# Turning the samples' attention sums by four transposes a head, with their quarters added in pairs by VectorE

## The reference, cut to what matters

```
s = einsum('bhik,bhjk->bhij', qc, kc) * w_intra
num = w_inter[..., None] * einsum('bhik,bhkv->bhiv', qc, C) + einsum('bhij,bhjv->bhiv', s, vc)
den = w_inter * einsum('bhik,bhk->bhi', qc, n) + sum(s, axis=-1)
h = num / maximum(abs(den), exp(-m_row))[..., None]
...
out = (sigmoid(o) * h_normed_by_head) @ w_out
```

## Time and profile before

| | |
|---|---|
| median of 3 runs | 2425.05 us (2423.37 to 2425.56) |
| time of the profiled execution | 2424.56 us |
| its span in the trace | 2422.4 us |
| PE busy, share of the span | 99% |
| DVE busy | 48% |
| ACT busy | 36% |
| POOL busy | 21% |
| granted TensorE clock, mean | 1.00 |

### The profile page before, as it was taken

The page is one execution under the profiler, slowest core; times in us unless marked ns, Lnnn a source line. Parts: engine busy times, 40 slices in busy tenths (PEclk is TensorE's granted clock), DMA queues, the critical chain, the costliest instruction groups (busy, mean ns, idle before and its releaser), DMA issues. The chain is left out here.

```text
span 2422.4 us, 43057 instructions
## 1 busy us (share of the span) xinstructions
PE 2409.2 (99%) x16236; PEld 2364.8 (98%) x16236; DVE 1160.7 (48%) x1332; ACT 877.0 (36%) x1048; POOL 509.6 (21%) x624
## 2 busy tenths in 40 slices
PE   9999999999999999999999999999999999999998
PEld 9999999999999999999988899999999999999997
DVE  6644444444434455544467875443444344434354
ACT  6333233333323333322445553333233333323332
POOL 7520022012101333210322113320022012101331
PEclk9999999999999999999999999999999999999999
DMA  6644554455445444545588764554554455445443
GB/s 237 176 150 151 151 148 148 148 149 153 147 147 149 149 144 147 146 145 152 160 275 270 250 194 139 157 148 150 152 149 148 148 149 152 149 147 148 147 152 113
DMA packets 198694, 389.68 MB, mean 161 GB/s; under 512 B 12229, under 2 KB 12485, under 8 KB 198153
## 3 DMA queue, kind: packets, MB, share of 16 engines
q1 hardware_dynamic: 197664, 385.78, 51.7%
q0 software_dynamic: 960, 2.94, 0.4%
HBM read 366.47 MB, written 22.66 MB: 161 GB/s over the span
## 5 line engine op out<-in xcount | busy, mean ns | idle before, releaser
L1108 DVE TENSOR_TENSOR w_lo<-w_raw,w_hi 128x1024 fp32r<-128x1024 f32 x648 | 829.4, 1282 | 1174.8 <-ACT w_hi L791 1157.9
L791 ACT ACTIVATE w_hi<-w_raw 128x1024 fp32r<-128x1024 f32 x608 | 644.4, 1061 | 1301.5 <-PE G L1589 1274.2
L1587 PE MATMUL G<-op_hi,w_hi 128*128 128x320 f32 x2816 | 873.6, 310 | 0.4 <-DVE qkv L1495 0.4
L1588 PE MATMUL G<-op_lo,w_hi 128*128 128x320 f32 x2816 | 868.6, 308 | 0.0
L1589 PE MATMUL G<-op_hi,w_lo 128*128 128x320 f32 x2816 | 868.6, 308 | 0.0
L1587 PE MATMUL G<-a_hi,w_hi 128*128 128x320 f32 x2304 | 710.9, 309 | 1.4 <-DVE hT L1227 0.8
L1589 PE MATMUL G<-a_hi,w_lo 128*128 128x320 f32 x2304 | 710.1, 308 | 0.0
L1588 PE MATMUL G<-a_lo,w_hi 128*128 128x320 f32 x2304 | 710.1, 308 | 0.0
L1587 PEld LDWEIGHTS G<-op_hi,w_hi 128*128 128x128 f32 x2816 | 528.2, 188 | 4.2 <-issue 1.3
L1588 PEld LDWEIGHTS G<-op_lo,w_hi 128*128 128x128 f32 x2816 | 528.2, 188 | 2.5 <-issue 1.0
L1589 PEld LDWEIGHTS G<-op_hi,w_lo 128*128 128x128 f32 x2816 | 528.1, 188 | 0.0
(11 more groups left out here) (253 smaller groups left out, 889.1 us busy)
## 6 DMA issues: line engine op xcount, KB each, us to landing
w_raw<-in_ffn_w_up SPq DMA_DIRECT2D x256, 512.0 KB, 3.7
w_raw<-in_ffn_w_down SPq DMA_DIRECT2D x256, 512.0 KB, 3.8
w_raw<-in_mlstm_w_in SPq DMA_DIRECT2D x96, 512.0 KB, 3.9
w_raw<-in_mlstm_w_out SPq DMA_DIRECT2D x32, 512.0 KB, 3.9
cst<-in_state_mlstm_C SPq DMA_DIRECT2D x26, 512.0 KB, 4.7
out_C_sample<-cst SPq DMA_DIRECT2D x26, 512.0 KB, 3.4
w_raw<-in_pool_w SPq DMA_DIRECT2D x8, 512.0 KB, 11.2
w_raw<-in_state_mlstm_C SPq DMA_DIRECT2D x6, 512.0 KB, 4.3
```

The source lines that it names most:

```text
L791: act.activation(w_hi[:, c % RING], w_raw[:, c % RING], ACT.Copy).then_inc(w_hi_ok, 1)
L1108: v.tensor_tensor(w_lo[:, slot], w_raw[:, slot], w_hi[:, slot].bitcast(F32), ALU.subtract).then_inc(w_lo_ok, 1)
L1587: pe.matmul(G[:, m, 0:T], w_hi[:, slot, t, w], hi[:, k, :], start=first and t == 0, stop=False)
L1588: pe.matmul(G[:, m, 0:T], w_hi[:, slot, t, w], lo[:, k, :], start=False, stop=False)
```

## The change

`samples_turned` no longer multiplies with `fold`. It transposes each 128 columns of `hs` against the identity, so that `X[2]` gets 4 blocks of 128 features by 128 columns (four quarters of 32) in place of 4 blocks of 64. `samples_out` takes the quarters apart: for each of the two parities (n = 0, 1) it copies the first quarter to `qkv` and adds the second quarter to it, and then multiplies by `rds` in place. A new semaphore, `fold_ok`, orders these steps. `fold` and its drawing on POOL go.

```diff
-        fold = sb("fold", [P, NS])
...
+        fold_ok = sem("fold_ok")
...
-            link(pool.memset(fold[:, :], 0.0))
-            for quarter in range(4):
-                select(by_quarter(fold[:, :])[:, quarter // 2], [[-TS, NSEQ // 2], [-1, TS]], 1, base=-quarter * GP,
-                       op=ALU.not_equal, fill=1.0)
...
             def samples_out(h):
 
                 v.wait_ge(x2_turned, h + 1)
-                v.tensor_tensor(att(h)[:, :, TP:T], X[2][:, 0:4 * NS].rearrange("p (a t) -> p a t", t=NS),
-                                bc(rds[:, :], [P, 4, NS]), ALU.mult).then_inc(att_s, 1)
+                turned = X[2][:, :].rearrange("p (a v t w) -> p v t a w", v=2, t=2, w=GP)
+                to = att(h)[:, :, TP:T].rearrange("p a (u v i) -> p v a u i", v=2, i=TS)
+                for n in range(2):
+                    first, second = (turned[:, n, t].rearrange("p a (u i) -> p a u i", i=TS) for t in range(2))
+                    v.tensor_copy(to[:, n], first).then_inc(fold_ok, 1)
+                    v.wait_ge(fold_ok, 4 * h + 2 * n + 1)
+                    v.tensor_tensor(to[:, n], second, to[:, n], ALU.add).then_inc(fold_ok, 1)
+                v.wait_ge(fold_ok, 4 * h + 4)
+                v.tensor_tensor(att(h)[:, :, TP:T], att(h)[:, :, TP:T], bc(rds[:, :], [P, 4, NS]), ALU.mult).then_inc(att_s, 1)
...
                 pe.wait_ge(hs_kept, h + 1)
                 for n in range(4):
-                    ins = pe.matmul(X[2][:, n * NS:(n + 1) * NS], hs[:, n * P:(n + 1) * P], fold[:, :], start=True, stop=True,
-                                    skip_group_check=True)
+                    ins = pe.transpose(X[2][:, n * P:(n + 1) * P], hs[:, n * P:(n + 1) * P], ident[:, :])
                 ins.then_inc(x2_turned, 1)
```

## The result

The changed kernel takes 2428.36 us (median of 22 runs, 2427.15 to 2429.66), the kernel before beside it 2424.87 us (22 runs, 2422.88 to 2427.80). The ratio is 1.0016 with a 95% interval of 1.0010 to 1.0022: +3.5 us, 0.14%. The forecast was 2427.9 us, or +2.9, with a range of 2423.4 to 2430.2: too small to tell apart from no change by the 0.2% that the prediction set, though with 22 runs a side the change is slower, and the interval leaves out 1.

A forecast was written before the change was run, and what follows sets the result against it. PE, busy 99%, was taken to bound the kernel, with the change's delays counted from DVE. 0.51 + 0.77 + 0.82 + 0.81 = +2.9 us on 2425.05 gave 2427.9 us, range 2423.4 to 2430.2.

The forecast's parts named there:

- The unit costs: At the turning, transposes hold PE 0.43 us against 0.84, sparing 0.41 a head; DVE's copies and additions are costed singly.
- c: DVE's added time a head ahead of the multiplication: 1.20 us, with bounds of 0.84 and 1.73.
- Rival 2: DVE's new pattern runs at half rate or its waits cost more: 1.73 us a head, 2430.1 us; chance 0.10.
- The places: PE would wait at L1841 for `att_s` (0.3 us), at L1809 in heads 1 to 3, and at chunk 3 after the last head.
- Rival 1: Update 0's idle time grows, so waits in heads 1 to 3 vanish: -0.4 us, or -1.6 at best; chance 0.15.
- Term by term: Delays at L1809 behind DVE's update 0: +0.51 us in head 1, +0.77 in head 2, +0.82 in head 3, adding to +2.10.
- DVE's idle time and the length of its instructions: No DVE idle time before update 0 in heads 1 to 3; four new instructions between 0.8 and 1.7 us.
- PE's sum of new waits: All new PE waits together: 4.5 us; a difference over 1.5 us would make the prediction wrong.
- After the last head: At chunk 3, PE waits for `w_lo`, delayed by DVE: +0.81 us, PE's saving included.
- PE waits for `hs` as now: After the last head, PE's wait for ACT's copy `hs` stays unchanged at 1.0 us.
- Rival 3: Transposes spare PE nothing; time is still +2.9 us because all four places count from DVE; inside the forecast.
- rival 4: PE's granted clock falls to 1.2 GHz; 5 us of work there gives about 2430 us; chance 0.02.

The follow-up runs named there:

- the exchange in chunk 0: Changed kernel with DVE's update 0 put ahead of `w_lo` in chunk 0 of heads 1 to 3: +2.1 us against before, ratio 1.0010.
- the second profile: Changed kernel run again unchanged, for a further profile: 2429.55 us, ratio 1.0019 to before.
- four more: Kernel before, products by `fold` kept, with the four new DVE instructions put ahead of its multiplication: +2.2 us, ratio 1.0008.
- eight more: Kernel before, products by `fold` kept, with eight extra DVE instructions a head ahead of its multiplication: +6.6 us, ratio 1.0027.
- turned twice: Changed kernel with its four transposes a head made twice in a row: +2.6 us against before, ratio 1.0011.
- transposes alone: Kernel before with four transposes a head replacing the products by `fold`, one DVE multiplication, adding of quarters left out: -0.9 us, ratio 0.9998.
- the update first in chunks 0 to 6: Changed kernel with DVE's update ahead of `w_lo` in chunks 0 to 6 of each head, chunk 7 left alone: +1.5 us against before, ratio 1.0009.
- the changed kernel with the update first: Changed kernel with DVE's update ahead of `w_lo` in all 8 chunks of all 4 heads: +2.7 us against before, ratio 1.0008.
- before, with the update first in all chunks: Kernel before with DVE's update ahead of `w_lo` in all chunks: -2.2 us, ratio 0.9991.

## Why the prediction was right, and where it was not

**The unit costs held.** Four transposes held PE for 0.43 us in head 1 and 0.41 after the last head (forecast from another line's transposes: 0.43). That this is saved in every head did not hold: in heads 2 and 3 PE's next weight load waits for DVE's last update, and 0.26 and 0.27 us were spared where the sum has 0.41. It did not change the total, because in these heads the sum counts from DVE. The Trainium skill's 275 ns in "TensorE: Matmul & The Clock Gate", Part 4, is the length of the record here as well (272 ns); as a cost it does not agree with this trace, in which they start 0.11 us apart. c was 1.16 us (forecast 1.20): copy 0.28, addition 0.29, and the copies started 0.20 us after the addition before them. Rival 2, the new pattern at half rate, fell with that.

**The places held.** PE waits for `att_s` 0.39 us (forecast 0.3) and at L1811, and DVE's idle time ahead of the update is gone. Rival 1, that the room holds, fell: `w_lo` beside POOL's squares took 2.02 us again. That only DVE counts there was shown by the transposes made twice, and that the order of update and `w_lo` is what carries it by the exchange in chunk 0. Term by term, by the second L1860 after each turning: head 1 +0.45 (forecast +0.51), head 2 +0.69 (+0.77), head 3 +0.73 (+0.82), together 1.87 us where 2.10 was forecast. Of the signs that the prediction named for itself, DVE's idle time and the length of its instructions came out as said. The third was PE's sum of new waits, forecast at 4.5 us within 1.5: what PE spares and what it loses (0.41 us and the delay of L1811) come to 0.8 us in head 1 and 1.0 in heads 2 and 3, where 0.9 and 1.2 were forecast, but the waits that the view lists at L1843 and L1811 are 1.9 us in total. Only with what the wait for `hs` is longer by, which was not forecast, and the two waits behind it in the second profile, is the list 2.8 to 3.6 us in the first profile and 3.7 to 4.5 in the second.

**After the last head,** +0.81 was forecast for chunk 3. In the second profile D is 0.1 shorter and E 0.8 longer, 0.7 together, with the two waits that were named. In the first the clock fell: D is 1.15 us longer than in the second and E 0.8 shorter, since PE came later to chunk 3 and did not wait there.

**What the sum left out: 1.4 us in C, by the average of two profiles each.** The step that failed is "PE waits for `hs` as now". It waited for 2.7 and 2.9 us, against 1.0 and 1.8. The prediction took that wait for an ending; the chain of waits shows that it is fed by a loop that begins behind L1811 of the last head, with chunk 1's update: update, store, weight load, `w_hi`, `w_lo`, the next update but one. In the changed kernel (start us, us, what), and then the three loads in the kernel before:

```profile
1366.52 0.38 SPq L469
...
1366.95 5.84 DMA w_raw<-in_mlstm_w_in
...
1372.81 1.07 ACT w_hi L795
...
1373.90 1.23 DVE w_lo L1104
...
1377.72 1.23 DVE cst L1502 x2
...
1379.39 4.38 DMA w_raw<-in_mlstm_w_in
...
1387.96 5.30 DMA w_raw<-in_mlstm_w_out
```

```profile
1366.10 4.57 DMA w_raw<-in_mlstm_w_in
...
1377.28 4.57 DMA w_raw<-in_mlstm_w_in
...
1386.04 4.70 DMA w_raw<-in_mlstm_w_out
```

The loads take part in it three times, and they account for the whole of the wait: in each of the nine profiles that have this chain, PE's wait for `hs` is the sum of the three loads less 12.8 us, to 0.02 us. In the changed kernel 5.84 + 4.38 + 5.30 = 15.52, and the wait is 2.70; in before 4.57 + 4.57 + 4.70 = 13.84, and it is 1.04. DVE's delay does not enter, since the loop and PE both start from L1811. So C is longer by head 3's 0.7 and by what the loads take longer.

The first load took 5.84 and 5.76 us in the changed kernel's profiles, against 4.57 and 4.77 in before's; the third took 5.3 and 5.5 against 4.7 and 5.0, the second 0.2 to 0.4 less. The same first load took 4.88, 4.54 and 4.83 us in the runs with four more, eight more and turned twice, and 5.98 and 5.61 in transposes alone and in the changed kernel with the update first in chunk 0. So, among the kernels that keep before's order in the last chunks, it is long in the four profiles (of three kernels) that turn with four transposes and short in the five (of four kernels) that turn with the products by `fold` or with eight transposes, so the transposes as such are not the reason. The last head's store of the prompt state (column "store") parts the fourteen profiles the same way: 3.0 to 3.9 us in the seven with a short turning, 4.5 to 5.3 in the seven with a long one. From L1811 on, the issues of the changed kernel and of the one with four more on DVE lie within 0.02 us of each other until the store, so the issues do not tell the two groups apart.

One thing in the transfers does: a single packet of 16 KB in the queue that the profile calls "instruction". Before, in the 5.1 us of the store (the busy tenths of the 16 DMA engines in 40 slices, then the queue's packets, MB and share of the 16 engines), and the changed kernel in the 5.8 us of the first weight load:

```profile
DMA  2989999999998989998521010118999998999999
q8 instruction: 1, 0.02, 2.1%
```

```profile
q8 instruction: 1, 0.02, 1.0%
```

In the seven profiles with the long store the packet comes 1.2 to 1.8 us after the store's issue. In the seven with the short one it comes 3.1 to 6.5 us after it, when the store has landed or all but landed, and in the time of the weight load. In before it took 2.1% of 16 engines' 5.1 us, or 1.7 us of one engine, the store is 1.7 us longer than the changed kernel's, and in the slices above the DMA engines fall to one tenth or less, the store waiting for its last part. The load is 4.5 to 5.1 us in the seven profiles that have the packet ahead of it, and 5.5 to 6.3 in the seven that have it inside. In six of these seven the two state loads also start earlier behind the weight load, 2.6 us after it and not 2.7 to 3.6, which may add to it; but in the changed kernel with the update first in chunks 0 to 6 they start 3.8 us after it and the load still takes 5.5 us, and with eight more on DVE 2.7 us after it and it takes 4.5.

By this the 1.1 us come from a fetch of instructions that fell on the load in place of the store; all fourteen profiles agree with it, but no run moved the packet by itself. Why it comes later where the turning has 4 matmuls and 4 weight loads in place of 8 and 8 is not shown. That the packet holds PE's own instructions, 24 fewer of them by the last head, would do it, and nothing here tests this. Nor was a reason found for the third load's 0.5 us.

That accounts for four more on DVE (+2.2) and turned twice (+2.6) being below the changed kernel (+3.5 and +4.2): they lose the forecast's terms and not the load's. The forecast of +2.9 was thus for what those two kernels do, and the total for the changed kernel came 0.6 to 1.3 us short: the terms were 0.3 us too large together, and the wait for `hs` was put at no change and was 1.4 us longer on average. That the miss was small is in part luck, since the place of the packet was nothing that the prediction had looked at. Rival 3 said that a change that spares PE nothing would cost the same; by the transposes made twice it costs slightly less, in one set of runs, and the intervals overlap. The profiles put the difference in the wait for `hs`.

**The clock** (rival 4, 0.02) was costed at nothing behind transposes, and is nothing right behind them: in heads 1 to 3 one profile of the fourteen shows a fall, in head 1 of the changed kernel with the update first, and there it came behind a wait of 1.5 us at `att_s`, 7 us after the transposes. Otherwise it fell behind PE's idle time for `hs`, in 4 of 7 profiles with 1.5 us or more of it, in none of the 7 with 1.2 us or less, before's second profile among the four. In before it cost 1.5 us. In the changed kernel D and E together are only 0.35 us longer with the fall than without it, because the waits for DVE behind it were gone. A longer wait for `hs` makes it at least not rarer; how often it fell in the unprofiled runs is not known.

**Faster than the kernel before by the median:** before, with the update first in all chunks, 2422.69 us against 2424.86 us beside it; by its interval (0.9982 to 1.0000) a gain of up to 0.2%, or none.

## What to carry to other kernels

An engine that is busy 99% of the time does not make every saving on it a gain: look at each place where it next meets the other engines, and read from the releasing engine's idle time how much room there is. Here 0.3 to 0.6 us of idle time and 0.04 us of slack behind it decided that 1.2 us on a half-idle VectorE cost more than 0.4 us on TensorE was worth. Look for such places on the way to the saving too: here PE met VectorE's last update as soon as it came 0.3 us earlier. And where a wait ends a stage, follow the chain behind it through the transfers before writing "as now", and look whether another queue has a packet in their time.

## What the runs showed of the hardware that I had not expected

- TensorE idle for 1.5 to 2.9 us between dense products: in 4 profiles of 7 the granted clock was 0.50 for some 3 us soon after, and the products 0.27 us apart in place of 0.15. An idle time of 2.9 us left it at 1.00 in another profile of the changed kernel. Of three waits of 1.5 us in one profile, the first was followed by a fall and the other two were not.
- A store of 512 KB took 3.0 to 3.9 or 4.5 to 5.3 us at the same place, by kernel and not by execution, and a load of the same size issued 3 us after it 4.5 to 5.1 or 5.5 to 6.3 us. In each of the fourteen profiles a 16 KB packet of the instruction queue lies in the time of one of the two, and that one took its longer time and the other its shorter one.
